# Two transformer blocks in one kernel: the scan's step projection moved behind attention head 3, the value projection wrapped around the last head, and one sum of squares moved to VectorE

## The reference

```python
x = x + 0.5 * _rmsnorm(_swiglu(_rmsnorm(x, ffn1_pre_g), ffn1_w_gu, ffn1_w_down), ffn1_post_g)
h = _rmsnorm(x, mix_pre_g)
q, k, v, z, xbc, dt_raw, gate_logits = jnp.split(h @ w_in, cuts, axis=-1)
...
o = _diff_attention(q, k, v, lam)                    # 8 heads, causal, two softmaxes a head
o = _rmsnorm(o, da_subln_g, SUBLN_EPS) * (1.0 - lam_init)
attn_out = o.transpose(0, 2, 1, 3).reshape(b, s, DA_V) @ w_branch_attn
...
dt = jax.nn.softplus(dt_raw + ssd_dt_bias)
a = -jnp.exp(ssd_A_log)
y = _ssd_chunked(xh * dt[..., None], a * dt, bm, cm) # the scan: needs cumulative sums of a * dt
...
g_attn, g_ssd = jnp.split(jax.nn.sigmoid(gate_logits + b_gate), N_BRANCH, axis=-1)
mixed = (g_attn * attn_out + g_ssd * ssd_out) @ w_mix_out
```

## Time and profile before

| | |
|---|---|
| median of 3 timed runs | 2709.05 us (2707.08 to 2709.09) |
| profiled execution, its own time | 2700.78 us |
| its span | 2699.0 us |
| mean granted TensorE clock | 0.99 |
| PE busy | 2606.6 us (97%) |
| PEld busy | 2142.1 us (79%) |
| DVE busy | 1361.6 us (50%) |
| ACT busy | 1130.1 us (42%) |
| HBM traffic | 93 GB/s over the span |

### The profile page before, as it was taken

The page is one execution under the profiler, slowest core; times in us unless marked ns, Lnnn a source line. Parts: engine busy times, 40 slices in busy tenths (PEclk is TensorE's granted clock), DMA queues, the critical chain, the costliest instruction groups (busy, mean ns, idle before and its releaser), DMA issues. The chain is left out here.

```text
span 2699.0 us, 34142 instructions
## 1 busy us (share of the span) xinstructions
PE 2606.6 (97%) x12712; PEld 2142.1 (79%) x12712; DVE 1361.6 (50%) x1998; ACT 1130.1 (42%) x1756; POOL 130.7 (5%) x96
## 2 busy tenths in 40 slices
PE   7998999999999999999999988999999999999997
PEld 5886777878888888888877766888877888888887
DVE  7553544344444444443655554777744454644424
ACT  5444544232322233232555544666642443522322
POOL 1000000010000000001000000111100201000001
PEclk9999999999999999999999998999999999999999
DMA  3212111223223322324421213333322332323234
GB/s 121 71 63 75 63 65 59 93 86 101 93 97 92 97 97 93 101 90 117 143 79 63 77 49 96 125 118 118 102 102 94 117 102 71 102 93 101 91 101 124
DMA packets 74270, 252.38 MB, mean 94 GB/s; under 512 B 8384, under 2 KB 11456, under 8 KB 74032
## 3 DMA queue, kind: packets, MB, share of 16 engines
q1 hardware_dynamic: 74160, 250.89, 28.8%
HBM read 248.69 MB, written 2.16 MB: 93 GB/s over the span
## 5 line engine op out<-in xcount | busy, mean ns | idle before, releaser
L201 PE MATMUL acc<-h_hi,w_hi 128*128 128x512 f32 (+1 forms) x2176 | 871.6, 401 | 20.2 <-PEq L233 9.0
L156 ACT ACTIVATE w_hi<-w_raw 128x1024 fp32r<-128x1024 f32 (+1 forms) x444 | 463.9, 1045 | 1015.1 <-PE acc L203 978.7
L203 PE MATMUL acc<-h_hi,w_lo 128*128 128x512 f32 (+1 forms) x2176 | 843.3, 388 | 0.0
L202 PE MATMUL acc<-h_lo,w_hi 128*128 128x512 f32 (+1 forms) x2160 | 836.5, 387 | 0.0
L167 DVE TENSOR_TENSOR w_lo<-w_raw,w_hi 128x1024 fp32r<-128x1024 f32 (+1 forms) x444 | 539.2, 1214 | 528.5 <-ACT w_hi L156 527.7
L201 PEld LDWEIGHTS acc<-h_hi,w_hi 128*128 128x128 f32 x2176 | 409.9, 188 | 124.7 <-issue 38.2
L203 PEld LDWEIGHTS acc<-h_hi,w_lo 128*128 128x128 f32 x2176 | 409.7, 188 | 85.2
L202 PEld LDWEIGHTS acc<-h_lo,w_hi 128*128 128x128 f32 x2160 | 407.3, 189 | 82.9 <-issue 5.3
L201 PE MATMUL acc<-9_hid_hi,w_hi 128*128 128x512 f32 (+1 forms) x440 | 156.1, 355 | 5.2 <-DVE w_lo L167 5.2
L202 PE MATMUL acc<-9_hid_lo,w_hi 128*128 128x512 f32 (+1 forms) x440 | 153.8, 350 | 0.0
L203 PE MATMUL acc<-9_hid_hi,w_lo 128*128 128x512 f32 (+1 forms) x440 | 153.8, 350 | 0.0
(11 more groups left out here) (435 smaller groups left out, 3510.0 us busy)
## 6 DMA issues: line engine op xcount, KB each, us to landing
w_raw<-in_w_gu SPq DMA_DIRECT2D x132, 512.0 KB, 3.4
w_raw<-in_w_down SPq DMA_DIRECT2D x60, 512.0 KB, 3.5
w_raw<-in_w_ssd SPq DMA_DIRECT2D x40, 512.0 KB, 3.5
w_raw<-in_w_swa SPq DMA_DIRECT2D x28, 512.0 KB, 3.4
w_raw<-in_w_gla SPq DMA_DIRECT2D x24, 512.0 KB, 3.4
w_raw<-in_w_da SPq DMA_DIRECT2D x24, 512.0 KB, 3.4
w_raw<-in_w_ssd_out SPq DMA_DIRECT2D x24, 512.0 KB, 3.4
w_raw<-in_w_xa SPq DMA_DIRECT2D x24, 512.0 KB, 3.4
```

The costliest lines, as they stand in the source:

```text
L156: c.nc.scalar.activation(c.w_hi[:, k % 2, 0:chunks * P], c.raw[:, k % 2, 0:chunks * P], ACT.Copy).then_inc(c.hi_done, 1)
L201: pe.matmul(out, hi, x_hi[:, j, cols], start=first, stop=False)
L202: pe.matmul(out, hi, x_lo[:, j, cols], start=False, stop=False)
L203: return pe.matmul(out, lo, x_hi[:, j, cols], start=False, stop=final)
```

## The change

There are three parts.

1. The squares of the first half are added up on DVE, 7 additions in place 0 of `9_up_hid`, and PE sums the one result (`sum_of_squares`) inside the first unit; the second half stays as it was. The mean of the second half of y is taken two chunks earlier. `root_of_x` stands on ACT behind the high split of the v unit instead of ahead of it, and DVE splits that unit before it waits for the root.
2. The projection of the scan's steps becomes two units of four chunks (`dt`) in the stream, behind the gate unit of head 3. Each half gets its own bank `acc` and is scaled into `15_x` and `15_e`. The exponentials stand in head 4, the logarithm in head 5, the rest of the DVE steps at the ends of heads 4, 5 and 6, and the store to memory on SP ahead of the load that is issued when k of head 7 has been split.
3. The last head's transposes, outputs and mean square stand between the chunks of value units 0 and 1; the last chunk (7) of both comes after them, then `last_rows`, then units 2 to 7 with nothing between. The normalised input is made two row tiles at a time beside units 2 to 5.

```diff
-            if KC * m + j >= 4:
-                act.wait_ge(x_squares_used, KC * m + j - 3)
-            act.activation(square_place(KC * m + j), at, ACT.Square).then_inc(x_squared, 1)
+            if m == 0 and j >= 4:
+                act.wait_ge(x_added, j - 3)
+            if m == 1:
+                act.wait_ge(x_squares_used, max(j - 2, 1))
+            act.activation(square_place(m, j), at, ACT.Square).then_inc(x_squared, 1)
@@ halves
+            if m == 0 and j >= 4:
+                dve.wait_ge(x_squared, j - 2)
+                if j > 4:
+                    dve.wait_ge(x_added, j - 4)
+                dve.tensor_tensor(square_place(0, 0), square_place(0, 0), square_place(0, j - 3), ALU.add).then_inc(x_added, 1)
@@ first_units
-                if (n, m, j) == (0, 0, 5):
+                if (n, m, j) == (0, 0, 3):
                     mean_of_y(pe, 1)
+                if (n, m, j) == (0, 0, 6):
+                    sum_of_squares(pe)
@@ branch_units
+    at = order.index(("gate", STEPS_BEHIND)) + 1
+    order[at:at] = [("dt", 0), ("dt", 1)]
@@ sync
-            if k == places["value", KC - 2]:
+            if k == places["k", H - 1]:
                 steps.store(sp)
@@ tensor
+            if g == STEPS_BEHIND:
+                for n in range(2):
+                    at, k = slice(n * KC // 2, (n + 1) * KC // 2), places["dt", n]
+                    multiply_tile(c, pe, 0, k, k, [(c.h_hi[:, at, :], c.h_lo[:, at, :])])
+        value_chunks(0, (0, 1))
+        for n in (0, 1):
+            att.transpose_tile(pe, H - 1, (H - 1) % 2, n)
+        value_chunks(0, (2, 3, 4))
+        for n in (2, 3):
+            att.transpose_tile(pe, H - 1, (H - 1) % 2, n)
+        value_chunks(0, (5, 6))
+        value_chunks(1, (0,))
+        outputs(H - 1)
+        value_chunks(1, (1, 2))
+        mean_square(H - 1)
+        value_chunks(1, (3, 4, 5, 6))
+        steps.turn(pe)
+        value_chunks(0, (7,))
+        value_chunks(1, (7,))
         pe.wait_ge(att.read, H * att.n + 2)
-        steps.project(pe, turn(H - 1))
-        outputs(H - 1)
-        mean_square(H - 1)
-        for j in range(4):
-            value(j)
-        pe.wait_ge(att.pt_done, att.turns + H * NT)
-        steps.turn(pe)
-        value(4)
         steps.last_rows(pe)
-        for j in range(5, KC):
+        for j in range(2, KC):
             value(j)
@@ scalar
+            if g == STEPS_BEHIND + 1:
+                steps.exponentials(act)
+            if g == STEPS_BEHIND + 2:
+                steps.logarithm(act)
...
+        for j in range(KC):
             weights_hi(j, "value")
-            high(j)
+            if j == 0:
+                steps.tables(act)
+            if j == 2:
+                steps.end_table(act)
+            if 2 <= j < 6:
+                high(2 * j - 4)
+                high(2 * j - 3)
@@ vector
+            if g == STEPS_BEHIND:
+                for n in range(2):
+                    k = places["dt", n]
+                    wait_tile(c, dve, 0, k)
+                    steps.take_half(dve, n, c.acc[k % 2]).then_inc(c.acc_free[k % 2], 1)
+                    wait_evacuated(c, dve, 0, k)
+                    dve.sem_inc(steps.halved, 1)
+                    weights_lo(n, "dt")
+                steps.argument(dve)
+            if g == STEPS_BEHIND + 1:
+                steps.steps_to_log(dve)
+            if g == STEPS_BEHIND + 2:
+                steps.steps_beside_log(dve)
+            if g == STEPS_BEHIND + 3:
+                steps.steps_to_sums(dve)
```

More of the change, by code:

```diff
@@ L1856, in load @@
     def load(self, sp):
-        for to, src in zip((self.raw, self.keep, self.last), self.sources):
+        for to, src in zip((self.keep, self.last), self.sources):
             sp.dma_start(to[:], src).then_inc(self.tables_in, 16)
@@ L1861, in store @@
         sp.wait_ge(self.dve_done, 9)
-        sp.dma_start(self.scratch.rearrange("g j h s -> (g j h) s"), self.sums[:]).then_inc(self.stored, 16)
-    def project(self, pe, between):
-        pe.wait_ge(self.lo_done, 1)
-        for k in range(KC):
-            w = slice(k * P, (k + 1) * P)
-            pe.matmul(self.proj[:], self.hi[:, w], self.c.h_hi[:, k, :], start=k == 0, stop=False)
-            pe.matmul(self.proj[:], self.hi[:, w], self.c.h_lo[:, k, :], start=False, stop=False)
-            mm = pe.matmul(self.proj[:], self.lo[:, w], self.c.h_hi[:, k, :], start=False, stop=k == KC - 1)
-            if k == KC - 1:
-                mm.then_inc(self.projected, 1)
-            between(k)
+        sp.dma_start(self.scratch.rearrange("g j h s -> (g j h) s"), self.sums).then_inc(self.stored, 16)
     def turn(self, pe):
@@ L1917, in tables, with end_table @@
         act.activation(tok[:, :, WHOLE], self.grouped(self.whole[:, 0:NT * H]), ACT.Exp).then_inc(self.tok_done, 1)
+    def end_table(self, act):
+        tok = self.tok
         act.wait_ge(self.dve_done, 10)
@@ L1966, in source, with branch_programs @@
         return a["w_da"][g // 2, 3 * (g % 2) + ("q", "k", "v").index(n)]
-    return ([(KC, lambda i, n=n, g=g: source(n, g)) for n, g in order],
+    return ([(KC // 2 if n == "dt" else KC, lambda i, n=n, g=g: source(n, g)) for n, g in order],
             {u: k for k, u in enumerate(order)})
-def branch_programs(c, ctx, stream, following, places, y_hi, y_lo, causal, gain, part, steps, root_x, banks, lam, first_units):
+def branch_programs(c, ctx, stream, following, places, y_hi, y_lo, causal, gain, part, steps, root_x, banks, lam, first_units, x_root):
     phase = (stream, following, c.unit, c.tile)
@@ L1996, in branch_programs @@
     normed = [att.s[0][m][:, n * S:(n + 1) * S] for m in range(2) for n in range(2)]
-    steps = SsdSteps(c, ctx, *steps, (*att.score, *att.turn),
-                     [to[0:SSD_HEADS, par, :] for to in (q, k_) for par in range(2)], root_x)
+    steps = SsdSteps(c, ctx, *steps, (*att.turn, att.score[0]), root_x)
     def gpsimd(pool):
@@ L2158, in scalar @@
         y_split(H - 1)
-        for j in range(2):
+        for j in range(KC):
             weights_hi(j, "value")
-            high(j)
-        steps.logarithm(act)
-        for j in range(2, 5):
-            weights_hi(j, "value")
-            high(j)
-        steps.tables(act)
-        for j in range(5, KC):
-            weights_hi(j, "value")
-            high(j)
+            if j == 0:
[5 more added lines that the diff above has]
+                high(2 * j - 3)
     def vector(dve):
@@ L2266, in vector @@
         dve.wait_ge(att.turned, (2 + H - 1) * NT)
-        for j in range(2):
+        for j in range(KC):
             product(j)
-            normalize(j)
-            if j > 0:
-                low(j - 1)
-        steps.steps(dve)
-        for j in range(2, 5):
-            product(j)
-            normalize(j)
-            low(j - 1)
-        steps.to_end(dve)
-        for j in range(5, KC):
-            product(j)
-            normalize(j)
-            low(j - 1)
-        low(KC - 1)
+            if j == 1:
+                steps.to_end(dve)
+            if 2 <= j < 6:
+                normalize(2 * j - 4)
+                normalize(2 * j - 3)
+                low(2 * j - 4)
+                low(2 * j - 3)
     return Programs(sync, tensor, scalar, vector, gpsimd)
```

128 lines of the change are left out of this document (66 added, 62 removed).

## The result

| | before | changed kernel |
|---|---|---|
| timed, 5 runs each | 2707.08 us (2699.77 to 2709.09) | 2689.05 us (2686.41 to 2690.71) |
| profiled execution, its own time | 2700.78 us | 2690.71 us |
| its span | 2699.0 us | 2688.9 us |
| mean granted clock | 0.990 | 0.992 |

The ratio is 0.9934 [0.9923, 0.9945]: faster, by 18.0 us. Over all undisturbed runs of this study the medians are 2707.0 (78 runs) and 2689.7 (17 runs), so 17.3 us. The forecast was 2695.5, in a range from 2690.5, and 13.5 us of gain. But between the two profiled executions there are only 10.1 us. Both distances want an explanation, one too large and one too small.

What follows compares the result with a forecast made beforehand. PE was taken as the bound, busy nearly throughout, losing time to waits and the clock behind them. 12.3 - 1.3 + 0.9 + 1.6 = 13.5 us gained: 2687.3 profiled, 2695.5 timed, range 2690.5 to 2701.5.

Steps and rivals of the forecast that it cites:

- The timed median is 2709.05, 8.3 above the profiled one, and the difference should carry over.: Whole kernel: the 8.3 us between profiled and timed execution is added to the profiled forecast of 2687.3, giving 2695.5.
- A wait of that size by itself costs only itself: Last head's copies: the clock reads 1.00 across PE's 2.79 us wait, so such a wait loses no clock.
- Tail, 12.3: Behind the last head: 12.9 of waits, 3.6 of clock and 2.0 at stage change gained, 6.2 of new waits: 12.3 us.
- Stage change, 2.0 and nothing for the clock: End of the stage: PE's idle time goes from 4.88 to 2.84 us, 2.0 gained within the tail, no clock gained.
- Part 2, -1.3: Half units of the projection behind head 3: PE waits 1.3 us for the split of q of head 4.
- Trunk, 0.9: Trunk's end, squares added on DVE: 0.9 us gained, bounds -3.1 and 3.0, part of PE's saving becoming longer waits.
- Root and mean, 1.6: Trunk's end: earlier mean of y gains 0.7 us and the 0.88 wait on v's low split goes, together 1.6.
- The clock's: Tail: clock falls behind the 2.2 and 2.7 waits, 1.6 to 2.0 us each; gain 10 to 12, about 2698; chance 0.17.
- DVE as the bound: Trunk's last phase: additions delay low splits, 0.9 becomes up to -3.1; gain 9.5 to 11.5, about 2699; chance 0.10.
- The load behind the moved store: Last head's gate unit: its load waits behind SP's store of the sums, kernel slower, about 2716; chance 0.03.
- the moved waits: Last head: interleaving makes ACT and DVE late, some 10 us come back, about 2705, no measurable change; chance 0.05.
- more is gained: Stage change keeps its clock (1.9 more) and all 3.0 of squares count: gain 17 to 18, about 2691; chance 0.13.

Runs made afterwards that it cites:

- q_split_first: `copies_first` with the high split of q of head 4 on ACT moved ahead of the table load and value copy: 2685.51 us, 0.9915 of before.
- sq_on_pe: Changed kernel with the first half's squares summed on PE again by eight ones matmuls, no DVE additions: 2692.05 us, 0.9946 of before.
- copies_first: Changed kernel with ACT's value copy and transposed-probability copies ahead of the gate's sigmoid and table loads, last head only: 2684.99 us, 0.9920 of before.
- copies_first_2: `copies_first` run and profiled once more, no further edit: 2686.08 us, 0.9913 of before.

## Why the prediction missed

The time came out 6.45 us below 2695.5 and 1.45 below the low end of the range. By its own steps:

**The step that failed: "The timed median is 2709.05, 8.3 above the profiled one, and the difference should carry over."** It did not. The profiled execution of before was nearly the fastest of all (2700.78; of the 78 others one was below, 2699.77), and that of the changed kernel was 1.66 above its median. So 8.3 + 1.66 = 9.9 us were wrong in this step. The other way went 3.4: the changed kernel's profile was at 2690.7, not 2687.3. 9.9 - 3.4 = 6.5, which is the miss. The further profiles bear it out: the first span of before (2699.0) is 5.1 us under the mean of its six (2704.1), while the first of the changed kernel (2688.9) is at the mean of its four. What the 8.3 were made of can be seen in the later profiles: falls of the clock in the tail, which the first execution happened not to have (78.0 us against 80.0 on average), the late load of 4.4 us in every second one, and 2 us by which a median of three runs lay above that of all 78.

**"A wait of that size by itself costs only itself"** was read from one window of the earlier trace rows, and is false as a rule. It held in that execution, but four of six of before lose the clock behind that very wait. It also hid part of the gain: the old tail costs 1.9 us more on average than the one I worked from.

Term by term, with the means of the six and the four profiles:

- *Tail, 12.3.* Measured 80.0 - 62.4 = 17.6 from `turn_v` of head 7 to the next stage, less the projection's 5.6 us, which moved: 12.0. The new waits are 5.6 instead of 6.2 (+0.6); the clock falls behind two of them (-2.9 on average: 3.3 in three profiles, 1.7 in one); and before loses more than its first profile (+1.9). 12.3 + 0.6 - 2.9 + 1.9 = 11.9. The sum came out right by luck: two errors of opposite sign, 2.9 and 2.5.
- *Stage change, 2.0 and nothing for the clock.* The wait came out at 2.83 for 2.84. The stage behind it takes 338.4 before and 337.4 after: another 1.0 us. By windows of 2 us the clock stays low for 4 to 5 us behind the restart in before, 3 in the changed kernel. That is read from the profiles alone; no run took the end of the stage by itself.
- *Part 2, -1.3.* 235.14 - 228.10 = 7.0, less 5.6: -1.4, nearly right, and the cause shown by `q_split_first`. The other moved steps cost PE no wait that the profile shows, as said.
- *Trunk, 0.9.* 1.7 by the whole phase, 1.4 by its second half. The mechanism was right (`sq_on_pe`); about half of the sums' time turned into waits, not two thirds.
- *Root and mean, 1.6.* 1.7 in every profile that has the edit.
- *Rivals.* The clock's came true, at the low end of its 1.6 to 2.0 us each, and the time was still lower, since the old tail had the same weakness. So the dips in the value units, a stated sign of being wrong, were there. DVE as the bound: not seen, the splits that PE waited for stood behind loads and not behind additions. The load behind the moved store and the moved waits: not seen. The lowest case, "more is gained", gave a time near the measured one, for other reasons.

Together the changed stretches and the start of the next stage give 12.0 + 1.0 - 1.4 + 1.7 + 1.7, 14.9 before rounding, for the forecast's 13.5. Another 1.5 on average is the late stretch; unchanged stretches elsewhere take 1.0 back; spans differ by 15.3 in the mean. Timed it is 17.3.

**What stays open.** Whether the late load is rarer in the changed kernel or was so by chance: three of six against none of four does not settle it, and I made no run that moves that stage alone. The last 2 us between profiles and timed medians are within what ten profiles can tell of runs that scatter over 13 us in before and 9 in the changed kernel. Why the clock falls behind one 2.1 or 2.8 us wait and not behind the same wait in another execution was not found. It is not the work ahead of it: from v of head 0 to `turn_v` of head 7 all six executions of before take 228.1 us and wait 2.78 to 2.81 behind it. That leaves the moment at which the wait comes; no run moved it on purpose.

## What to carry to other kernels

Before a sum is made against one profiled execution, compare its own time with the timed runs: where it is among the fastest, look for what it lacks (a fall of the clock, a late load), and don't carry the distance over. Price a wait of 2 us or more on a busy TensorE at its length plus a good chance of another 1.7 us, in the old kernel as in the new: behind the waits of 2.7 to 2.8 us the clock fell in 10 of 13 profiles, behind those of 2.1 in 7 of 9. And when a wait is the last large one in its stretch, look first at what stands ahead of its releaser: here a sigmoid whose result was needed some 55 us later (1586.7 and 1642.1 in the changed kernel) stood with its two table loads ahead of the copies, and moving it shortened the tail from 62.8 us by 4.5 or by 6.1, depending on whether the clock fell behind the next wait.

## What the runs showed of the hardware

- In 18 profiles the clock lost in the tail is 1.7, 3.4, 5.1, 8.5, 10.2 or 11.9 us, always at 0.50 of full speed, the lower of its two levels; one fall behind a wait of 2 to 3 us costs 1.7. The same wait (2.78 to 2.81 us in before, 2.71 to 2.73 in the changed kernel, 2.08 to 2.10 at the last rows) was followed by such a loss in some executions and by 1.00 in others. Shorter waits can do it too: `copies_first` and `copies_first_2` lost as much behind 1.82 and 1.88 us on a low split near 1293, while `q_split_first` lost none behind 1.89 us near 1275. The Trainium skill, TensorE: Matmul & The Clock Gate, Part 1, has the clock as throttled by default and released by activity; these runs agree in so far as, in the stretches read here, it only fell at or behind idle time.
- A table load and its successor: in `copies_first` the load starts at 1587.79, lasts 1.28 us, and the sigmoid starts at 1589.09. The Trainium skill, ScalarE: Activation LUTs, "What ACT_TABLE_LOAD costs", adds some 1380 ns of draining at a switch to a different set. No run here shows it: at this switch the copy ahead of the load ends at 1587.78, and the sigmoid starts 0.02 behind it. The load ahead of the last rows is of the set already in place, so the Trainium skill's price for a switch, which the prediction applied there, does not bear on it; they waited 2.10 us for the 2.2 forecast without it.
